# Context projections of all recurrent heads unsplit in the delta-rule stage, layer 0's modulation ahead of it

## The reference, cut to what matters

```python
sh_c, sc_c, gt_c = adaln(c_ctx, ada_w[i], ada_b[i])          # "modulation": silu(c) @ ada_w + ada_b
h_ctx = rms_norm(x_ctx, norm_g[i]) * (1.0 + sc_c) + sh_c
qc, kc, gc, vc, zc = hgrn_project(h_ctx, w_in, lb)           # here only f (2 directions) and v are needed
ql, kl, gl, vl, zl = hgrn_project(h_lat, w_in, lb)
o_cf, s_cf = chunk_scan(qc, kc[0], vc, gc[0], s0)            # s_cf: end state, forward
o_cb, s_cb = chunk_scan(flip(qc), flip(kc[1]), flip(vc), flip(gc[1]), s0)
o_lf, _ = chunk_scan(ql, kl[0], vl, gl[0], s_cf)
o_lb, _ = chunk_scan(flip(ql), flip(kl[1]), flip(vl), flip(gl[1]), s_cb)
```

## Time and profile before

| | us |
|---|---|
| three runs, median | 2090.73 |
| span of the profiled execution | 2095.0 |
| projection stage, 24 to 198.5 | 174.5 |
| delta-rule stage, 198.5 to 383 | 184.5 |
| feed-forward, 440 to 843 | 403 |
| 16 heads, 898 to 1608 | 710 |

### The profile page before, as it was taken

The page is one execution under the profiler, slowest core; times in us unless marked ns, Lnnn a source line. Parts: engine busy times, 40 slices in busy tenths (PEclk is TensorE's granted clock), DMA queues, the critical chain, the costliest instruction groups (busy, mean ns, idle before and its releaser), DMA issues.

```text
span 2095.0 us, 35679 instructions
## 1 busy us (share of the span) xinstructions
PE 1987.7 (95%) x15123; PEld 1596.7 (76%) x15123; DVE 1274.9 (61%) x2191; ACT 811.5 (39%) x1267; POOL 0.2 (0%) x4
## 2 busy tenths in 40 slices
PE   6998888899999999999999999999998799999998
PEld 5876556667788787788888888888887585887876
DVE  6622776555536566577777777777777634343343
ACT  4364333533324433634343344434344224332333
POOL 0000000000000000000000000000000000000000
PEclk9999888999999999999999999999999799999999
DMA  5331212325435333221212111221211131223221
GB/s 175 92 83 38 82 63 82 92 90 167 135 115 157 100 86 87 71 61 51 61 52 62 51 52 53 60 61 52 61 52 51 36 115 41 70 81 91 81 81 51
DMA packets 286160, 164.68 MB, mean 79 GB/s; under 512 B 6348, under 2 KB 283570, under 8 KB 286002
## 3 DMA queue, kind: packets, MB, share of 16 engines
q1 hardware_dynamic: 285492, 162.22, 26.2%
q10 hardware_dynamic: 510, 0.18, 0.0%
HBM read 160.29 MB, written 2.10 MB: 78 GB/s over the span
## 4 chain that ended last, share of the span: by engine, by line
PE 87%; DVE 7%; ACT 3%; issue 2%; DMA 1%; ACTq 0%; SPq 0%; DVEq 0%
PE bank L481 21%; PE bank L483 20%; PE bank L482 20%; PE bank L498 2%; PE bank L499 2%; PE bank L500 2%; PE bank L895 2%; PE bank L1036 1%; PE bank L943 1%; PE bank L926 1%; PE bank L464 1%; PE bank L903 1%; PE bank L519 1%; PE bank L673 1%; DMA stage<-in_w_up 1%
## 5 line engine op out<-in xcount | busy, mean ns | idle before, releaser
L481 PE MATMUL bank<-hh,wh 128*128 128x512 f32 x1384 | 565.2, 408 | 0.0
L1622 DVE TENSOR_TENSOR wl<-stage,wh 128x1024 fp32r<-128x1024 f32 (+1 forms) x246 | 298.3, 1214 | 434.3 <-ACT wh L1107 434.2
L1107 ACT ACTIVATE wh<-stage 128x1024 fp32r<-128x1024 f32 (+1 forms) x246 | 257.6, 1049 | 767.0 <-PE bank L483 466.5
L483 PE MATMUL bank<-hh,wl 128*128 128x512 f32 x1384 | 542.7, 392 | 0.0
L482 PE MATMUL bank<-hl,wh 128*128 128x512 f32 x1384 | 542.5, 392 | 0.0
L481 PEld LDWEIGHTS bank<-hh,wh 128*128 128x128 f32 x1384 | 260.9, 189 | 58.3 <-issue 6.4
L483 PEld LDWEIGHTS bank<-hh,wl 128*128 128x128 f32 x1384 | 261.1, 189 | 57.0
L482 PEld LDWEIGHTS bank<-hl,wh 128*128 128x128 f32 x1384 | 261.7, 189 | 48.4 <-issue 1.0
L481 PE MATMUL bank<-gh,wh 128*128 128x512 f32 x416 | 166.3, 400 | 16.7 <-DVE gl L1930 7.2
L482 PE MATMUL bank<-gl,wh 128*128 128x512 f32 x416 | 164.6, 396 | 0.0
L483 PE MATMUL bank<-gh,wl 128*128 128x512 f32 x416 | 164.3, 395 | 0.0
(11 more groups left out here) (379 smaller groups left out, 2699.4 us busy)
## 6 DMA issues: line engine op xcount, KB each, us to landing
stage<-in_hg_w_in SPq DMA_DIRECT2D x80, 512.0 KB, 3.6
stage<-in_ada_w SPq DMA_DIRECT2D x48, 512.0 KB, 3.8
stage<-in_w_up SPq DMA_DIRECT2D x44, 512.0 KB, 5.0
stage<-in_ft_w_in SPq DMA_DIRECT2D x32, 512.0 KB, 3.9
stage<-in_w_in SPq DMA_DIRECT2D x28, 512.0 KB, 3.8
stage<-in_w_down SPq DMA_DIRECT2D x16, 512.0 KB, 4.0
stage<-in_hg_w_out SPq DMA_DIRECT2D x16, 512.0 KB, 4.0
stage<-in_ft_w_out SPq DMA_DIRECT2D x16, 512.0 KB, 3.9
```

The costliest lines, as they stand in the source:

```text
L481: pe.matmul(bank[t % NLIN][:], wh[:, s, k, :], xh[:, k, :], start=a, stop=False)
L483: mm = pe.matmul(bank[t % NLIN][:], wl[:, s, k, :], xh[:, k, :], start=False, stop=b)
L1107: do(A.activation(wh[:, l % NSPLIT, 0:nk, :], stage[:, u["slot"], 0:nk, :], ACT.Copy), "hi_ready")
L1622: do(X.tensor_tensor(wl[:, l % NSPLIT, 0:nk, :], stage[:, u["slot"], 0:nk, :], wh[:, l % NSPLIT, 0:nk, :].bitcast(F32), ALU.subtract), f"s ...
```

## The change

- The 48 projections of the context (3 units x 16 heads) become plain float32 products straight from `stage`, without `high` and `weight_low`. They leave the head stage and are put into the delta-rule stage, two steps for each head: part 0 and part 1 of step n (`context_work`). The 48 weight units are loaded a second time for it.
- The decays, keys and end states of the context follow there too: sigmoid on ScalarE, `context(g)` on VectorE, `ctx_keys` and `ctx_state` on TensorE. Each end state goes to a buffer in HBM (128 KB) and all 16 come back in one transfer `S0` of 2 MB ahead of the feed-forward; the head stage reads them there.
- `ctxtok` is loaded in the projection stage, turned behind tiles 24 to 27 and normed there; the feed-forward's second round loses this work.
- Layer 0's modulation, 12 pairs of raw units, goes from the steps of the delta rule to behind tiles 2, 4, .. 16, 20, .. 26 of the projection stage, its columns two tiles later.
- In the head stage the scan's points are moved: `turn_values` after tile t, then at the slices counted in `PLACES` over the 32 slices of tiles t+1 .. t+4: levels 0 and 1 after 1, levels 2 to 7 after 3, 6, 10, 14, 19, 23, `turn_keys` after 25, `chunk_states` and `inside` after 27, `output` after 30.

```diff
...
+PLACES = (1, 3, 6, 10, 14, 19, 23, 25, 27, 30)
+MOD_TILE = {(2 if j < 8 else 4) + 2 * j: j for j in range(12)}
+MOD_COLUMNS = {min(t + 2, 27): j for t, j in MOD_TILE.items()}
...
         add("w_in", (0, 8), t * P if t < 16 else O_B + (t - 16) * P, "h")
-    units.extend(raws[:24])
+        if t in MOD_TILE:
+            units.extend(raws[2 * MOD_TILE[t]:2 * MOD_TILE[t] + 2])
+    for hd in range(HG):
+        for s in (1, 2, 3):
+            units.append(dict(w="hg_w_in", rows=(0, 8), col=s * E_IN + hd * P, lin=False, ctx=(hd, s)))
...
+            def store_state(g):
+                sp.wait_ge(S("cx_ev"), CTX_AT[g, "st"] + 1)
+                if g:
+                    sp.wait_ge(S("st_out"), 16 * g)
+                sp.dma_start(states_out[:, g, :], stc[:, g % 2, :, :].rearrange("p d c -> p (d c)")).then_inc(S("st_out"), 16)
...
+                if u["lin"] and u["w"] == "w_in" and u["tile"] == 8:
+                    sp.dma_start(ctxtok[:], d["ctx_2"][0].rearrange("(a p) c -> p a c", p=P)).then_inc(S("ctx_in"), 16)
+                if "ctx" in u and u["ctx"][1] == 3 and u["ctx"][0] >= 3:
+                    store_state(u["ctx"][0] - 3)
+                if u["w"] == "w_out" and u["tile"] - T_OUT in (2, 3, 4):
+                    store_state(HG - 5 + u["tile"] - T_OUT)
...
-                    sp.dma_start(ctxtok[:], d["ctx_2"][0].rearrange("(a p) c -> p a c", p=P)).then_inc(S("late_in"), 16)
+                    sp.wait_ge(S("st_out"), 16 * HG)
+                    sp.dma_start(S0[:], states_out.rearrange("p g (d c) -> p g d c", d=2)).then_inc(S("late_in"), 16)
...
-                if u["ctx"]:
-                    next(between, None)
-                    ci = 3 * ((t - T_HG) // 5) + (t - T_HG) % 5 - 1
-                    half = [0, CT, 0][ci % 3]
-                    if ci == 0:
-                        pe.wait_ge(S("ada1"), 1)
-
-                    if ci:
-                        pe.wait_ge(S("cevac"), ci)
-                    for k in range(nk):
-                        a, b = k == 0, k == nk - 1
-                        o = bank[7][:, half:half + CT]
-                        pe.matmul(o, wh[:, s, k, :], ch[:, k, :], start=a, stop=False)
-                        pe.matmul(o, wh[:, s, k, :], cl[:, k, :], start=False, stop=False)
-                        mm = pe.matmul(o, wl[:, s, k, :], ch[:, k, :], start=False, stop=b)
...
+            def ctx_f(g, dr):
+                u = units[pos[0]]
+                assert u["ctx"] == (g, 1 + dr)
+                pos[0] += 1
+                if g == 0:
+                    pe.wait_ge(S("cx_h"), KT)
+                    pe.wait_ge(S("ada_done"), 1)
+                pe.wait_ge(S(f"stage_in{u['slot']}"), 16 * (u["load"] + 1))
+                o = ctx_room(g, ("f0", "f1")[dr])
+                for k in range(KT):
+                    mm = pe.matmul(o, stage[:, u["slot"], k, :], ctxh[:, k, :], start=(k == 0), stop=(k == KT - 1))
+                mm.then_inc(S(f"stage_free{u['slot']}"), 1)
+            def ctx_v(g):
+                u = units[pos[0]]
+                assert u["ctx"] == (g, 3)
+                pos[0] += 1
+                pe.wait_ge(S(f"stage_in{u['slot']}"), 16 * (u["load"] + 1))
+                o = ctx_room(g, "v")
+                for a in range(2):
+                    for k in range(KT):
+                        mm = pe.matmul(o[:, a * P:(a + 1) * P], ctxh[:, k, a * P:(a + 1) * P], stage[:, u["slot"], k, :],
+                                       start=(k == 0), stop=(k == KT - 1))
+                mm.then_inc(S(f"stage_free{u['slot']}"), 1)
+            def ctx_keys(g):
+                pe.wait_ge(S("kq_rdy"), g + 1)
+                for dr in range(2):
+                    o = ctx_room(g, ("k0", "k1")[dr])
+                    for a in range(2):
+                        mm = pe.transpose(o[:, a * P:(a + 1) * P], kcx[:, dr, a * P:(a + 1) * P], ident[:])
+                    mm.then_inc(S("cx_pe"), 1)
+            def ctx_state(g):
+                pe.wait_ge(S("cx_ev"), CTX_AT[g, "k1"] + 1)
+                o = ctx_room(g, "st")
+                for dr in range(2):
+                    for a in range(2):
+                        mm = pe.matmul(o[:, dr * P:(dr + 1) * P], ctok[:, dr, a, :], vct[:, g % 2, a, :],
+                                       start=(a == 0), stop=(a == 1))
+                mm.then_inc(S("cx_pe"), 1)
+            def context_work(n, part):
+                g = n // 2
+                if n % 2 == 0 and part == 0:
+                    if g >= 2:
+                        ctx_state(g - 2)
+                    ctx_f(g, 0)
+                elif n % 2 == 0:
+                    ctx_f(g, 1)
+                elif part == 0:
+                    ctx_v(g)
+                elif g:
+                    ctx_keys(g - 1)
...
                 attention_tail(n)
+                context_work(n, 0)
...
                 scores(n + 1)
-                modulation(n)
+                context_work(n, 1)
...
+            def ctx_take(g, what, dst):
+                if what in ("f0", "f1", "v"):
+                    u = ctx_unit[g, {"f0": 1, "f1": 2, "v": 3}[what]]
+                    act.wait_ge(S(f"stage_free{u['slot']}"), u["load"] + 1)
+                else:
+                    act.wait_ge(S("cx_pe"), CTX_PE[g, what])
+                do(A.activation(dst, ctx_half(g, what), ACT.Copy), "cx_ev")
+            def take_keys(g):
+                ctx_take(g, "k0", ctok[:, 0, :, :].rearrange("p a c -> p (a c)"))
+                ctx_take(g, "k1", ctok[:, 1, :, :].rearrange("p a c -> p (a c)"))
+            def take_state(g):
+                if g >= 2:
+                    act.wait_ge(S("st_out"), 16 * (g - 1))
+                ctx_take(g, "st", stc[:, g % 2, :, :].rearrange("p d c -> p (d c)"))
+            def context_ahead(n):
+                g = n // 2
+                if n % 2:
+                    ctx_take(g, "f1", sgc[:, g % 2, 1, :])
+                elif g >= 2:
+                    take_keys(g - 2)
+            def context_behind(n):
+                g = n // 2
+                if n % 2 == 0:
+                    if g >= 2:
+                        take_state(g - 2)
+                        act.wait_ge(S("kq_rdy"), g - 1)
+                    ctx_take(g, "f0", sgc[:, g % 2, 0, :])
+                else:
+                    ctx_take(g, "v", vct[:, g % 2, :, :].rearrange("p a c -> p (a c)"))
+                    do.settle()
+                    do(A.activation(sgc[:, g % 2, :, :], sgc[:, g % 2, :, :], ACT.Sigmoid), "cx_sig")
...
+            def context_behind(n):
+                if n and n % 2 == 0:
+                    context(n // 2 - 1)
...
+                        s_in = S0[:, h, dr, :] if a == 3 * dr else ST[:, dr, a, :]
+                        mm = pe.matmul(bank[6][:, a * P:(a + 1) * P], s_in, KK[:, dr, a * P:(a + 1) * P],
...
-                context_state(g)
                 level(g, 0)
                 level(g, 1)
                 yield
-                yield
-                for li in range(2, 6):
+                for li in range(2, 8):
...
+                    next(steps, None)
                     for i in range(1, 5):
-                        next(steps, None)
-                        units_to(t + i, ("h_ready", 3 * KT) if h == 0 and i == 1 else None, steps)
+                        units_to(t + i, ("h_ready", 2 * KT) if h == 0 and i == 1 else None, steps,
+                                 [p - KT * (i - 1) for p in PLACES])
...
```

More of the change, by code:

```diff
@@ L111, in make_units, with add @@
     units, tiles = [], []
-    def add(w, rows, col, x, start=True, stop=True, ctx=False, back=0):
+    def add(w, rows, col, x, start=True, stop=True, back=0):
         if start:
@@ L512, in whole_tile @@
                 u = units[pos[0]]
-                assert u["lin"] and u["tile"] == t and u["stop"] and not u["ctx"]
+                assert u["lin"] and u["tile"] == t and u["stop"]
                 pos[0] += 1
@@ L675, in weigh, with ctx_room @@
                 mm.then_inc(S("pv_done"), 1)
-            def modulation(step):
-                if step - 1 in MOD_STEP:
-                    mod_columns(MOD_STEP[step - 1])
-                if step in MOD_STEP:
-                    for _ in range(2):
-                        unit(units[pos[0]])
-                        pos[0] += 1
+            def ctx_room(g, what):
+                if CTX_ROOM[g, what]:
+                    pe.wait_ge(S("cx_ev"), CTX_ROOM[g, what])
+                if CTX_BANK[g, what] == 2:
+                    if weighed[0]:
+                        pe.wait_ge(S("ob_lo"), weighed[0])
+                    elif not CTX_ROOM[g, what]:
+                        pe.wait_ge(S("vb_ev"), TT)
+                return ctx_half(g, what)
@@ L1000, in _ @@
                     for n in range(EARLY):
-                        unit(units[pos[0]], heads_in if n == 0 else None, steps, slots=range(KT))
+                        unit(units[pos[0]], heads_in if n == 0 else None, steps, slots=(2, 4, 6, 8))
```

(1 more changed line is left out.)

341 lines of the change are left out of this document (179 added, 162 removed).

## The result

The changed kernel takes **2247.7 us** (median of 4 runs, 2239.9 to 2252.2) against 2091.3 of the kernel before (4 runs, 2090.7 to 2094.3): a ratio of 1.072, 95% interval 1.070 to 1.075. It is slower, as forecast, but the range ended at 2222 and the forecast was 2175.

A forecast was written before the change was run, and what follows sets the result against it. Taken as bound by TensorE in heads and projection stage, with air only in the delta-rule stage. 21 + 2 + 141 - 4 + 1 - 77 = +84 on a span of 2095.0, scaled to 2175 us; 8-in-10 range 2120 to 2222.

The forecast's parts named there:

- Projection stage, +21 and +2: Projection stage: modulation adds 1.75 us for each of twelve tile pairs, +21; the context's turning adds transposes and seams, +2.
- Delta stage, 325 us: Delta-rule stage: becomes bound by TensorE, 292 us of its work plus 28 and 5 of waits, 325 us, +141.
- 28 forecast for softmax and states: Delta-rule stage: TensorE waits 0.8 us for the softmax and 0.95 ahead of `ctx_state` per head, 16 x 1.75 = 28.
- heads and tails: Delta-rule stage: starts and ends of the four chunks cost 8 us together, about half covered by context work: 5.
- The table's switch: Delta-rule stage: a sigmoid table load of 1.28 us within ScalarE's 3.0 us after odd steps; `ctx_state` waits about 0.95.
- my 103: Delta-rule stage: TensorE's own work at full clock, 154.3 busy less modulation's 16.6 and 8.5 and 26 us that would vanish.
- less half of the time at half clock: Delta-rule stage: mean clock 0.86 means 28% of 184.5 us at half rate, so 26 us of work would vanish.
- Feed-forward, -4 and +1: Feed-forward: 16 transposes with seams and two sums go, -4; the larger `S0` transfer costs +1, ends 0 and +6.
- Heads, -77: Head stage: a head falls to about 44.0 us; 15 heads -65, head 0 -8.6, drain behind head 15 -3.
- The three waits: Each head: TensorE waits 2.4 us at level 2, 2.4 at level 4, and 0.45 at `chunk_states` for ScalarE.
- rival C: Heads: the clock falls behind each of two long waits, 1.7 us lost each, +51 in all: 2226 us; chance 0.12.
- Rival A: Heads stay bound by TensorE at 37.85 us each, so the kernel is faster, 2050 to 2083 us; chance 0.08.

The follow-up runs named there:

- the order mended: Changed kernel with ScalarE making the high of the weights at the end of its work in projection tiles 16 to 27: 2227.7 us.
- the later points: Changed kernel with the scan's levels 2 to 7 after slices 7, 10, 15, 19, 24, 27, the rest after 30 and 32: 2140.0 us.
- all fixes: Changed kernel with ScalarE's highs late in projection tiles 16 to 27, scan points later, the last two after slices 29 and 31: 2110.1 us.
- the 208.1 without it: Kernel before with only layer 0's modulation moved behind the projection stage's tiles: 2156.6 us, delta stage 208.1 us.
- one wait of 2.42 us a head: Changed kernel with VectorE's low of the weights behind tile t+1 made after produce 4 instead of 3: 2195.1 us.
- one of 1.74 us: Changed kernel with VectorE's produce 2 ahead of the low behind tile t, and the low behind t+1 after produce 4: 2191.2 us.

## Why the prediction was wrong, step by step

- **What bounds which stage** of the kernel before was right: the heads by TensorE, air only in the delta stage. Plain products cost TensorE more than split ones (L763 3.46 us for its 16 instructions, L775 3.57 for 32; worked out 3.48 and 3.55), and all rests on how much air they fill.
- **Projection stage, +21 and +2: failed.** Measured +45.9. The step that failed is "The loads (two raw units and two tiles in 12.5 us) are as dense as in the feed-forward, where this price already holds their waits." The density was right (126 GB/s in this stage) and the conclusion wrong: behind tiles 16 and up ScalarE has other work behind the `high` that waits for a load, and TensorE needs that work. With the order mended the stage costs +25.3, which is the forecast's sum. I priced the loads and never read ScalarE's list of this stage against them.
- **Delta stage, 325 us: right in sum, not in terms.** Measured 331.8 by the forecast's bounds (337.6 less the 5.8 by which these landmarks lie wider). The waits were too dear: 28 forecast for softmax and states, 15.3 measured (L721 7.0, L785 and L794 7.4, others 0.9: the sum of TensorE's waits between 246 and 580 us); heads and tails 5, as measured (L825 2.6, L908 2.5). The table's switch was the mis-sized one (0.17 a head). TensorE's own work at full clock was too cheap: 331.8 - 189 - 21 = some 122, between my 103 and the upper end 129. Part of these 19 us is the context's: by the distances between starts, waits taken out, its instructions cost 198 us in the stage and not 189. The other part is the step "less half of the time at half clock": the clock did come to 0.98, and the stage's own work still did not shrink to 103. Why is open. That the errors of 13 and 19 nearly cancel is luck.
- **Feed-forward, -4 and +1: failed by 6.** Measured +3.1 between the whole tiles. The same stretch, with the same code, took 411.1 to 414.8 us in the eight experiments on the changed kernel; in the four on the kernel before, with its code, it took 410.6 to 415.8. So executions differ by more than the saving of 4 that was forecast, and it cannot be told from none.
- **Heads, -77: failed by size.** Measured -45.5 with head 0 and the rest. The three waits (2.4, 2.4, 0.45 forecast; 2.42, 2.30, 0.36 measured) were right to a tenth of a microsecond; the smaller ones forecast at levels 1 and 6 (0.4, 0.7) did not appear. With the base of a whole head without waits (38.3: 38.98 with the later points, less its wait of 0.67; forecast 37.85) they make 43.4 us, where 44.0 was forecast. Measured are 46.1. The step that failed is the one that put the clock at nothing in this sum: stretches at the 1.2 GHz level, 1.45 us each and three in two heads, make 2.2 of the 2.7 us; the other 0.5 is open. The term was rival C's, priced near (1.7 us for every wait; 1.45 measured, behind three of four) and given 0.12. Its 3.5 us at the lower level were no good reading of the place that it names: around the wait of the earlier trace rows the granted clock is 0.51 from 246.8 to 253.7 us. The argument against it, "between these waits the engine is full, and in the heads now the granted clock is 1.00", compared with a stretch that has no such waits. The last distance, which gained nothing where 4.3 was forecast, is the rest of the miss: without a head's tiles around it, TensorE waits for VectorE for some 10 us before the change and 9 after it.
- **Rival A** named the right cure for the heads at the right size ("levels 2 and 4 would have to stand 4 slices later"): with points 4 slices later for level 2 and 5 for level 4 a head costs 39.1 us. Its total was out of reach: with all fixes 2110.
- **The range** took in one large miss at a time. The 23 us of the projection stage and rival C's own 51 together carry 2175 to 2249. That the kernel stands there is luck: the clock's fall cost some 30 us in the 14 whole heads and not 51, and small misses in the last distance, the delta stage and the feed-forward fill the gap.

Why even the mended version loses: by the landmarks, the context costs the delta stage 128.7 us (336.8 less the 208.1 without it) and gives the heads back 156.6 (135.8 + 18.1 + 2.7), so this part gains 28. The modulation, with the context's turning, costs 25.6 us in the projection stage, and 17.8 in the delta stage that it left, 43 together. This counts the two moves in one order, modulation first; the 17.8 are the price of a clock of 0.71, and with the context in the stage the clock is 0.98, so in the other order the shares would differ. That the two can be had apart is not shown: the context's scale and shift come from that modulation, which so has to stand ahead of it, and no version with both in the delta stage was run.

## What to carry to other kernels

Before moving work out of a stage that has air, ask what it does there: work that TensorE does in its waits can hold its clock, and here taking 25 us of it away made the stage 17.8 us longer. Where loads are put into a ring, read each engine's program order behind the instruction that waits for them, and not only the bandwidth. And a wait of 2.4 us on an engine that is otherwise full is not its own length: here it cost some 1.45 us more in the clock, three times in four, so price it wherever the trace shows the lower level behind a wait of like length.

## What the runs showed of the hardware

- 26 us of useless TensorE work in the delta stage shortened it by 16 us (208.1 to 192.1) while the granted clock rose from 0.71 to 0.89; 44 us more in a stage at 0.86 raised it to 0.93 and lengthened the stage by 29.
- In the heads the clock fell to the 1.2 GHz level behind waits of 2.42 and 2.30 us, with TensorE full before and after, but not behind every one: 21 of 28 in the 14 whole heads. With one wait of 2.42 us a head it fell behind 8 of 14, with one of 1.74 us (and smaller ones of 0.48 and 0.83) behind 5 of 14, with 0.67 alone never. Each fall cost about 1.45 us.
- 31 table loads of 1.28 us on ScalarE, two in nearly every head, made 2.7 us of the delta stage's time, 0.17 a head; the activation behind such a load starts 0.01 us after its end.
